# First two activation tiles in column halves, the bias vector among the fillers, and the first weight cast on another engine

## The reference

```python
h = jnp.concatenate([meta, x], axis=1)          # 16 + 512 rows of 1024
h = layer_norm(h, ln_emb_g, ln_emb_b)
...
proj = h @ w_in                                 # (qa, ka, va, ga, qi, ki, wi, cq, ckv, kpe, gb)
...
bias = rel_bias[t5_bucket(t_pos[None, :, None] - sel)]
...
return layer_norm(ALPHA * h + out, ln_g, ln_b)
```

## Time and profile before

| | us |
|---|---|
| median of 3 runs (329.2 to 329.46) | 329.42 |
| the profiled execution | 329.67 |
| its span, first to last instruction | 327.9 |
| PE busy in the span | 317.0 (97%) |
| DVE busy | 237.0 (72%) |
| POOL busy | 196.4 (60%) |
| ACT busy | 173.0 (53%) |
| PE busy from 18.04 to 27.1 | 9.06 of 9.06 |

### The profile page before, as it was taken

How to read it: one execution, slowest core, us unless ns; L and a number is a source line. 1 busy time by engine, 2 the same in 40 slices (tenths; PEclk the granted TensorE clock), 3 DMA queues, 4 the chain that set the end, 5 groups by cost and what they waited for, 6 DMA issues and landing times.

```text
span 327.9 us, 6250 instructions
## 1 busy us (share of the span) xinstructions
PE 317.0 (97%) x2134; PEld 275.5 (84%) x2134; DVE 237.0 (72%) x630; ACT 173.0 (53%) x389; POOL 196.4 (60%) x243
## 2 busy tenths in 40 slices
PE   7899999999999999999999999999999999999991
PEld 6699987878778888987988988898978898998991
DVE  5984810279955799989995996478787866564786
ACT  4876843362442455367454754777586752822230
POOL 6562999989322262439430898789869582570222
PEclk9999999999999999999999999999999999999998
DMA  7564333239322122202300042322322211140033
GB/s 248 219 197 183 130 128 117 83 136 295 135 98 78 55 78 78 80 3 80 131 9 9 20 162 112 120 84 68 104 84 97 65 26 42 65 130 0 2 128 128
DMA packets 11997, 32.86 MB, mean 100 GB/s; under 512 B 2440, under 2 KB 2824, under 8 KB 11968
## 3 DMA queue, kind: packets, MB, share of 16 engines
q1 hardware_dynamic: 9232, 26.89, 23.1%
q10 hardware_dynamic: 2736, 5.59, 5.9%
HBM read 29.83 MB, written 4.81 MB: 106 GB/s over the span
## 4 chain that ended last, share of the span: by engine, by line
PE 90%; DVE 5%; ACT 1%; DMA 1%; issue 1%; ACTq 0%; DVEq 0%; SPq 0%
PE ps_j L1486 54%; PE ps_t L1486 8%; PE ps_o L1723 6%; PE ps_s L1674 6%; PE ps_s L1678 3%; PE ps_s L1647 3%; PE ps_t L1693 2%; PE ps_j L1540 2%; PE ps_t L1698 2%; PE ps_j L1563 1%; DMA res<-in_x 1%; PE ps_j L1441 1%; PE ps_j L1431 1%; DVE st L1037 1%; PE ps_j L1424 1%
## 5 line engine op out<-in xcount | busy, mean ns | idle before, releaser
L588 POOL TENSOR_TENSOR wl<-raw,wh 128x1024 fp32r<-128x1024 f32 (+2 forms) x33 | 78.1, 2374 | 46.3 <-ACT wh L595 46.1
L1486 PE MATMUL ps_j<-hh,wh 128*128 128x512 f32 (+2 forms) x208 | 72.9, 351 | 0.2 <-DVE qs L1158 0.2
L1486 PE MATMUL ps_j<-hl,wh 128*128 128x512 f32 (+2 forms) x208 | 72.4, 348 | 0.0
L1486 PE MATMUL ps_j<-hh,wl 128*128 128x512 f32 (+2 forms) x208 | 72.2, 347 | 0.0
L748 POOL TENSOR_SCALAR pr<-pr,rden 128x528 f32<-128x528 f32 (+1 forms) x64 | 35.1, 570 | 49.8 <-DVE rden L1299 49.8
L989 ACT ACTIVATE pr<-pr,mn 128x528 f32<-128x528 f32 (+1 forms) x64 | 36.0, 564 | 15.6 <-DVE mn L1288 15.6
L1486 PEld LDWEIGHTS ps_j<-hh,wh 128*128 128x128 f32 (+1 forms) x208 | 38.7, 186 | 6.2 <-issue 0.3
L1486 PEld LDWEIGHTS ps_j<-hh,wl 128*128 128x128 f32 (+1 forms) x208 | 38.8, 187 | 5.1
L1486 PEld LDWEIGHTS ps_j<-hl,wh 128*128 128x128 f32 (+1 forms) x208 | 38.7, 186 | 5.0
L595 ACT ACTIVATE wh<-raw 128x1024 fp32r<-128x1024 f32 (+2 forms) x34 | 34.9, 1038 | 0.2 <-DMA raw<-in_weights 0.2
L766 POOL TENSOR_TENSOR bm<-bias,mask 128x144 f32<-128x144 f32 (+3 forms) x32 | 27.5, 894 | 0.0
(11 more groups left out here) (287 smaller groups left out, 842.9 us busy)
## 6 DMA issues: line engine op xcount, KB each, us to landing
raw<-in_weights SPq DMA_DIRECT2D x35, 512.0 KB, 3.3
bias_by_distance<-bias_vector ACTq DMA_DIRECT2D x1, 2624.0 KB, 13.3
bias<-bias_by_distance ACTq DMA_DIRECT2D x8, 264.0 KB, 3.0
res<-in_x SPq DMA_DIRECT2D x4, 512.0 KB, 4.7
out<-res SPq DMA_DIRECT2D x3, 512.0 KB, 2.6
raw<-in_weights SPq DMA_DIRECT2D x5, 256.0 KB, 5.6
pt<-in_ln_emb_g SPq DMA_DIRECT2D x1, 512.0 KB, 5.4
pt<-in_ln_emb_b SPq DMA_DIRECT2D x1, 512.0 KB, 6.0
```

Source lines behind the costliest of these rows:

```text
L588: eng.tensor_tensor(ring_of(False, b), raw_of(b), ring_of(True, b).bitcast(F32), ALU.subtract).then_inc(done, 1)
L1486: last = pe.matmul(dst, a, b, start=n == 0 and part[0], stop=n == count - 1 and part[1])
```

## The change

- SP issues tiles 0 and 1 as four loads, left and right column halves in turn, with semaphores `x_right` for the right ones; the one-hot table goes ahead of them, tiles 2 and 3 behind the first weight halves, and gains and `rel_bias` leave SP's queue for ACT's.
- ACT makes the product of negated mean and reciprocal for meta and tile 0 too, and normalises in column halves (`normal(n, half, done)`); DVE's product of line 1049 is gone.
- DVE takes the statistics of tiles 2 and 3 later, in one piece each, and its reciprocals stand elsewhere.
- The first half of weight block 0 is cast by POOL, behind DVE's normalising of tile 1, instead of by ACT.
- PE makes the bias vector between the fillers, of which there are 16 and 7 instead of 30 and 6; the meta tile is transposed behind `spread(3)`, with its own semaphore `meta_t`, for which SP and DVE now wait; in the second half `low(2)` and `low(3)` stand one place earlier, and `spread(4)` waits for left halves alone.

The diff, without the renumbered waits of the last layer norm:

```diff
@@ -431,6 +431,7 @@
         ps_j = ctx.enter_context(nc.psum_tensor("ps_j", [P, 2, 512], F32))
 
         x_in = [sem(f"x_in{t}") for t in range(5)]
+        x_right = [sem(f"x_right{t}") for t in range(2)]
         par_in = sem("par_in")
         emb_in = sem("emb_in")
         tab_in = sem("tab_in")
@@ -448,7 +449,6 @@
         w_high = sem("w_high")
         w_high_dve = sem("w_high_dve")
         w_high_pool = sem("w_high_pool")
-        w_first_act = sem("w_first_act")
         xn_dve = sem("xn_dve")
         xn_act = sem("xn_act")
         center = sem("center")
@@ -577,7 +578,7 @@
         def high_made(eng, b):
 
             if b == FIRST_BLOCKS:
-                eng.wait_ge(w_high_pool, 3)
+                eng.wait_ge(w_high_pool, 4)
             else:
                 eng.wait_ge(w_high, b - FIRST_BLOCKS)
 
@@ -621,22 +622,21 @@
 
         @block.sync
         def _(sp):
+            def tile_in(t):
+
+                sp.dma_start(res[:, t, :], x[0, t * P:(t + 1) * P, :]).then_inc(x_in[t], 16)
+
             sp.dma_start(x_meta, meta).then_inc(x_in[4], 16)
-            def tile_in(t):
-
-                sp.dma_start(res[:, t, :], x[0, t * P:(t + 1) * P, :]).then_inc(x_in[t], 16)
-
-            tile_in(0)
-            tile_in(1)
-            sp.dma_start(gain[:, :], gains).then_inc(par_in, 16)
-            sp.dma_start(rb[:, :], rel_bias).then_inc(par_in, 16)
             sp.dma_start(oh_sb, onehot).then_inc(oh_in, 16)
-            tile_in(2)
+            for t in range(2):
+                sp.dma_start(res[:, t, 0:512], x[0, t * P:(t + 1) * P, 0:512]).then_inc(x_in[t], 16)
+                sp.dma_start(res[:, t, 512:1024], x[0, t * P:(t + 1) * P, 512:1024]).then_inc(x_right[t], 16)
             for half in range(2):
                 c = slice(4 * half, 4 * half + 4)
                 for b in range(FIRST_BLOCKS):
                     sp.dma_start(raw[:, b, c, :], weights[b, :, c, :]).then_inc(raw_in[b] if half else first_in[b], 16)
                 if half == 0:
+                    tile_in(2)
                     tile_in(3)
 
 
@@ -648,7 +648,7 @@
                     sp.dma_start(cos_sb[:, :], cos_t).then_inc(tab_in, 16)
                     sp.dma_start(sin_sb[:, :], sin_t).then_inc(tab_in, 16)
                 if b == 3:
-                    sp.wait_ge(x_t, 1)
+                    sp.wait_ge(meta_t, 1)
                     sp.dma_start(emb_g, ln_emb_g.partition_broadcast(P)).then_inc(emb_in, 16)
                     sp.dma_start(emb_b, ln_emb_b.partition_broadcast(P)).then_inc(emb_in, 16)
             sp.wait_ge(job_mm, NJ["tq", 2 * HEADS - 1, 0] + 1)
@@ -693,14 +693,17 @@
                                    wh[:, c, 0:2 * P].rearrange("p c (b n) -> p b c n", b=2).bitcast(F32),
                                    ALU.subtract).then_inc(w_low, 1)
 
-            pool.wait_ge(w_first_act, 1)
+            pool.wait_ge(xn_dve, 2)
+            pool.wait_ge(first_in[0], 16)
+            pool.tensor_copy(wh[:, 0:4, 0:P], raw[:, 0, 0:4, :]).then_inc(w_high_pool, 1)
+            pool.wait_ge(w_high_pool, 1)
             pool.wait_ge(w_high_dve, 1)
             first_low(0)
             first_low(1)
             for b in range(FIRST_BLOCKS):
                 pool.wait_ge(raw_in[b], 16)
                 pool.tensor_copy(wh[:, 4:8, b * P:b * P + P], raw[:, b, 4:8, :]).then_inc(w_high_pool, 1)
-            pool.wait_ge(w_high_pool, 2)
+            pool.wait_ge(w_high_pool, 3)
             first_low(2)
             first_low(3)
             pool.wait_ge(raw_in[2], 16)
@@ -713,7 +716,7 @@
 
                     t = arg[0] // 2
                     pool.wait_ge(emb_in, 32)
-                    pool.wait_ge(x_t, DC + 1)
+                    pool.wait_ge(x_t, DC)
                     if arg[0] % 2 == 0:
                         pool.tensor_tensor(res[:, t, :], res[:, t, :], emb_g, ALU.mult).then_inc(res_done, 1)
                     else:
@@ -791,24 +794,27 @@
 
             def negative(n):
 
-                t = TILES[n][0]
-                act.activation(nmr[:, t:t + 1], mv[:, t, 0:1], ACT.Copy, scale=-1.0).then_inc(center, 1)
-
-            def normal(n, need):
-
                 t, r = TILES[n]
-                src = x_meta if t == 4 else res[:, t, :]
-                act.wait_ge(shift, need)
-                if n > 2:
-                    act.wait_ge(center, 2 * n - 5)
-                    act.activation(nmr[:, t:t + 1], nmr[:, t:t + 1], ACT.Copy, scale=rstd[:, t:t + 1]).then_inc(center, 1)
-                    act.wait_ge(center, 2 * n - 4)
+                act.activation(nmr[0:r, t:t + 1], mv[0:r, t, 0:1], ACT.Copy, scale=-1.0).then_inc(center, 1)
+
+            def scaled_mean(n, done):
+
+                t, r = TILES[n]
+                act.wait_ge(shift, n + 1)
+                act.wait_ge(center, done - 1)
+                act.activation(nmr[0:r, t:t + 1], nmr[0:r, t:t + 1], ACT.Copy, scale=rstd[0:r, t:t + 1]).then_inc(center, 1)
+
+            def normal(n, half, done):
+
+                t, r = TILES[n]
+                src = (x_meta if t == 4 else res[:, t, :])[:, 512 * half:512 * half + 512]
+                act.wait_ge(center, done)
                 act.activation(src, src, ACT.Identity, bias=nmr[0:r, t:t + 1],
                                scale=rstd[0:r, t:t + 1]).then_inc(xn_act, 1)
 
             def gains_of(u):
 
-                act.wait_ge(x_t, u + 2)
+                act.wait_ge(x_t, u + 1)
                 for n, c in enumerate(unit(u)[0]):
                     half = hbank(u)[:, 256 * n:256 * n + 256]
                     act.activation(half, half, ACT.Identity, bias=bcol[:, c:c + 1],
@@ -824,26 +830,36 @@
                 act.activation(hh[:, chunks[0]:chunks[1] + 1, s], hbank(u).rearrange("p (c n) -> p c n", c=2),
                                ACT.Copy).then_inc(h_high, 1)
 
+            act.dma_start(rb[:, :], rel_bias).then_inc(par_in, 16)
+            act.dma_start(gain[:, :], gains).then_inc(par_in, 16)
             deviation(0)
-            normal(0, 2)
+            negative(0)
+            scaled_mean(0, 2)
+            normal(0, 0, 2)
             deviation(1)
-            normal(1, 4)
+            negative(1)
+            normal(0, 1, 2)
+            scaled_mean(1, 4)
             deviation(2)
-            act.wait_ge(first_in[0], 16)
-            act.activation(wh[:, 0:4, 0:P], raw[:, 0, 0:4, :], ACT.Copy).then_inc(w_first_act, 1)
+            normal(1, 0, 4)
+            normal(1, 1, 4)
             act.wait_ge(par_in, 32)
             gains_of(0)
             high(0)
+            high(1)
+            gains_of(2)
             deviation(3)
             negative(3)
-            high(1)
-            gains_of(2)
             high(2)
-            normal(3, 6)
+            scaled_mean(3, 6)
+            normal(3, 0, 6)
+            high(3)
+            normal(3, 1, 6)
             deviation(4)
             negative(4)
-            high(3)
-            normal(4, 7)
+            scaled_mean(4, 8)
+            normal(4, 0, 8)
+            normal(4, 1, 8)
             gains_of(4)
             high(4)
             high(5)
@@ -1034,21 +1050,20 @@
                 src = x_meta if t == 4 else res[:, t, :]
                 if half == 0:
                     dve.wait_ge(x_in[t], 16)
+                elif t < 2:
+                    dve.wait_ge(x_right[t], 16)
                 dve.bn_stats(st[0:r, t, half, :], src[0:r, 512 * half:512 * half + 512]).then_inc(bn_s, 1)
                 if half == 1:
                     dve.wait_ge(bn_s, 2 * n + 2)
                     dve.bn_aggr(mv[0:r, t, :], st[0:r, t, :, :].rearrange("p a b -> p (a b)")).then_inc(stats, 1)
 
-            def inverse(n, done):
+            def inverse(n):
 
                 t, r = TILES[n]
                 dve.wait_ge(root, n + 1)
                 dve.reciprocal(rstd[0:r, t:t + 1], rstd[0:r, t:t + 1]).then_inc(shift, 1)
-                dve.wait_ge(shift, done)
-                if n < 2:
-                    dve.scalar_tensor_tensor(out=nmr[0:r, t:t + 1], in0=mv[0:r, t, 0:1], scalar=-1.0,
-                                             in1=rstd[0:r, t:t + 1], op0=ALU.mult, op1=ALU.mult).then_inc(shift, 1)
-                elif n == 2:
+                if n == 2:
+                    dve.wait_ge(shift, 3)
                     for x in (0, 512):
                         part = res[:, t, x:x + 512]
                         dve.tensor_scalar(part, part, mv[:, t, 0:1], rstd[:, t:t + 1], ALU.subtract,
@@ -1056,7 +1071,7 @@
 
             def gains_of(u):
 
-                dve.wait_ge(x_t, u + 2)
+                dve.wait_ge(x_t, u + 1)
                 for n, c in enumerate(unit(u)[0]):
                     half = hbank(u)[:, 256 * n:256 * n + 256]
                     dve.tensor_scalar(half, half, gcol[:, c:c + 1], bcol[:, c:c + 1], ALU.mult,
@@ -1073,30 +1088,30 @@
             stat(0, 0)
             stat(0, 1)
             stat(1, 0)
-            inverse(0, 1)
+            inverse(0)
             stat(1, 1)
             stat(2, 0)
```

(48 more changed lines are left out.)

7 lines of the change are left out of this document (4 added, 3 removed).

## The result

The change makes the kernel **slower**: 330.70 us in the median of 12 runs against 329.44 (329.16 to 329.91, 12 runs) for the kernel before on the same chip. Its runs lie in two groups, eight from 330.32 to 330.91 and four from 332.63 to 332.78, and the profiled execution (span 330.9, its own time 332.78) is of the upper one; the lower group has no trace of its own. The prediction was 328.6, with a range of 328.2 to 329.7. One run of a later kernel, 394.8 us at a mean granted clock of 0.753 where all others have 0.977 or more, was in a slower state and is left out.

The account below looks back on a forecast made before the run. TensorE, solid behind 27 us, was taken to bound the kernel; its 21.24 group starting at 20.34 gives 0.90, less 0.12 for the walk's optimism: −0.78, so 329.42 becomes 328.64 us, range 328.2 to 329.7.

Parts of the forecast that it names:

- What bounds the kernel: TensorE is solid behind 27 us; only an earlier start of the second half's first weight product, at 21.24, gains.
- The copies: Loads at the start: tile 0's left half lands at 4.5, the next halves at 5.2, 5.9 and 6.6.
- Halves 0.7 apart: Landing spacing of tiles 0 and 1's column halves, taken from weight halves at 12.0 and 12.7.
- No half comes later than the whole tile did: Upper end for the landing of tile 0's left half: 4.83; that end gives a gain of 0.45.
- The rival of the late halves: Halves land 1.05 apart, tile 1's right half at 7.65: 329.0 to 329.8 us; chance 13%.
- VectorE up to the transposes: VectorE's statistics and normalising of tiles 0 and 1: first transposes start at 8.88 instead of 10.12.
- From there to the group: From the first transposes to the second half's first weight product: it starts at 20.34 instead of 21.24.
- 6.64 in one piece: VectorE's unbroken work from the gains at 10.03 to tile 3's reciprocal at 16.67, 0.25 later than before.
- DVE, with its weight cast done by then: VectorE's weight cast does not delay its first gains, which start at 10.03 instead of 11.48.
- The fewer fillers: nothing, except for the clock: Cutting TensorE's early fillers from 36 to 23 costs nothing unless the clock falls.
- The rival: TensorE idles 2.4 us before the first transposes, its clock falls: 1 to 2 us slower, 330 to 331; chance 9%.
- The port: POOL's weight cast beside VectorE's, sharing SBUF interfaces: at most 0.3 less gain, taken as 0.

Follow-up runs that it names:

- 16/30: The change with 30 instead of 7 filler transposes behind the bias vector's matmuls (16 ahead kept): 331.08 us, ratio 1.0055 to the kernel before.
- 30/20: The change with 30 instead of 16 fillers ahead of the bias vector's matmuls and 20 instead of 7 behind: 330.58 us, ratio 1.0033 to the kernel before.
- the square above: Table of copies by many or few fillers; kernel before 329.5 against 331.29 and 330.21; change's orders with copies of before 329.67 against 331.65.
- 16/7: The change itself, 16 fillers ahead of the bias vector's matmuls and 7 behind, against 30 and 6 in the kernel before: 330.70 us, ratio 1.0054.
- the kernel with the shortened piece: Change's orders, copies of before, 30 and 6 fillers, tile 3's statistics ahead of the second low part: 329.41 us, ratio 0.9996 to the kernel before.

## Why the prediction was wrong, point by point

- **What bounds the kernel: right.** TensorE behind 27 us is rigid; the delay of 2.96 at the 21.24 group comes out as 3.11 at the end, and 1.2 gained there as 0.97. In all 16 profiled executions the span is longer or shorter than 327.9 by what that group's start differs from 21.24, within 0.2.
- **The copies: wrong, the first step that failed.** "Halves 0.7 apart" gave 5.9 and 6.6 for tile 1; in the four profiled executions with these copies (the change twice, 16/30, 30/20) its halves landed at 6.7 to 7.3 and at 7.5 to 7.9. The prediction let a half land sooner behind its issue than a whole tile, but tile 1's right half took 4.5 to 4.8, no less than the whole tile 1 in most traces (4.2 to 5.3), and it is issued 0.94 later behind two more issues. "I put 4.5" for the left half of tile 0 was 5.33 in the change's trace, outside its own ends of 4.2 to 4.83, and 4.2, 4.5 and 5.6 in the other three: that one is spread. "No half comes later than the whole tile did" left out the tables moved at the same time; whether they matter beyond their slot of 0.45 is not shown, since without them ahead the last half landed at 7.0 and 7.1, and the slot alone would give 7.1 to 7.4. The rival of the late halves had named the spacing of 1.05 and the 7.65, and 7.71 came; its 13% was low.
- **VectorE up to the transposes: right as a walk, late by its inputs.** 8.88 became 9.93 in the profiled run and 9.71 at full clock. From tile 1's right half to the transposes the walk had 2.09, the two traces 2.20 and 2.19.
- **From there to the group: right in sum.** "6.64 in one piece" measured 6.46. "Left half 17.17 to 17.78" assumed half of a whole tile's 1.25; a half takes 0.80 to 0.81, and two together 1.51 against 1.24. From the first transposes to the group the walk had 11.46, and at full clock it took 11.48. So with the front late by 0.83 nothing of the 0.78 is left: 21.19 against 21.24.
- **"DVE, with its weight cast done by then": not tested by the change**, where the cast came at 10.15 without a wait. With an earlier front it waited 1.14 to 1.78 for its copy in three kernels where tile 2 went first, and 0.86 and 1.64 in two where four halves and small tables stood ahead of it. With a front as early as 8.27 it did not wait only where the tiles are whole and the weight halves go ahead of tile 2, issued from 3.52 on instead of 4.01 and 4.48. So the change's order of that copy is right, and its late front hid that.
- **"The fewer fillers: nothing, except for the clock": the step that decided.** The rival had the mechanism and the place (an idle stretch ahead of the transposes, matmuls at half rate behind it) and a price of 1 to 2 us, 330 to 331, which holds the lower group; the upper group is beyond it, since the level lasted 10.2 us instead of the 2.9 that the rival's walk took from the start of the kernel. Its chance of 9% was the real error. It rested on one row, full clock in an idle stretch of 4 us near the end, and one such row excludes nothing; read on, the same trace has the clock at 0.50 from 325.4 on, before that idle stretch is over (the two lines below this point). The start-up row spoke louder: with the granted clock's row at 1.00 the transposes took 421 ns. In the square above fewer fillers cost 0.7 to 2.0 us wherever the copies are those of before, and there by a late rise of the clock, which the rival did not name. With the change's copies the lower groups of 16/30 and 16/7 are 0.7 to 0.8 apart, so the late landings, which both have, are not what puts the change's lower group above it. The Trainium skill's TensorE: Matmul & The Clock Gate (What's actually happening) says that an idle array goes back to half rate, and that the number of slow matmuls at the start of one kernel differs from run to run; the trace agrees with both, with 2.52 us of idleness here and with 4.93 and 6.38 for the same 30 fillers in two kernels.

```profile
325.00:325.50 0.50, 0.00 (x0) 0.00 (x0) 0.36 (x2) 0.00 (x0) 0.00 (x0) 0.87 0.23 86
325.50:326.00 0.50, 0.00 (x0) 0.00 (x0) 0.00 (x0) 0.00 (x0) 0.00 (x0) 0.50 1.06 384
```

- **The port: nothing on VectorE.** Its cast took 0.42 beside POOL's, and 0.43 in the kernel with the shortened piece, where POOL stood idle. POOL's own took 0.74 in the change and 0.83 with the copies of before, where it runs beside VectorE's, and 0.61 alone. The range had 0.3 for this. The two operations compared in the earlier trace rows are of different lines; the one of 0.43 itself took 2.52 beside POOL at 36.0, so the row stands, but neither is a cast.

What stays open: the lower group of the change (eight of its first 12 runs, 330.3 to 330.9, mean clock 0.992 to 0.997) was never profiled. Its spans of 328.4 to 329.0 put its group at about 21.7 to 22.3, an estimate from the rule of spans above. That the cause is a late rise to full clock, as in the three kernels with 16 fillers and the copies of before (profiled at 330.37, 331.31 and 331.35), is argued and not shown. No kernel has the change's copies with 30 fillers ahead of the vector and 7 behind, so it is open which of the two counts matters there, and also why the array rises now 3 and now 12 us after its first filler.
